# The down projection of a decoder layer: ten sums of weight blocks move from GpSimd to VectorE, and the product of gate and up is made in row halves

## What is computed

```python
h = h + (jax.nn.silu(hn @ W['w_gate'][i]) * (hn @ W['w_up'][i])) @ W['w_down'][i]
gate = jax.nn.sigmoid(rmsnorm(h, W['g_ple'][i]) @ W['w_ple_gate'][i])
h = h + gate * (p[i] @ W['w_ple_proj'][i])
```

## Time and profile before

| | |
|---|---|
| median of 3 runs | 2861.48 us (2856.12 to 2864.07) |
| profiled execution | 2864.79 us, span 2863.0 us |
| busy shares of the span | TensorE 88%, VectorE 48%, ScalarE 25%, GpSimd 21% |
| mean granted TensorE clock | 0.939 of full speed |
| gate and up | about 1808 to 2379 us |
| down | about 2389 to 2698 us |
| embedding stage | about 2698 to 2863 us |

### The profile page before, as it was taken

The page is one execution under the profiler, slowest core; times in us unless marked ns, Lnnn a source line. Parts: engine busy times, 40 slices in busy tenths (PEclk is TensorE's granted clock), DMA queues, the critical chain, the costliest instruction groups (busy, mean ns, idle before and its releaser), DMA issues. The chain is left out here.

```text
span 2863.0 us, 35015 instructions
## 1 busy us (share of the span) xinstructions
PE 2525.2 (88%) x13920; PEld 1741.5 (61%) x13940; DVE 1374.0 (48%) x2301; ACT 706.9 (25%) x1387; POOL 611.8 (21%) x546
## 2 busy tenths in 40 slices
PE   6999999494789997887768779999999998999998
PEld 4555544152578786455445435688888887787743
DVE  0589999342567764586634113422222225334233
ACT  3222220052344453675423200111111110000011
POOL 2000000102544431400056502222122211202000
PEclk9999999695799999898889879999999999999999
DMA  7111101702245443514889843011101104110211
GB/s 267 49 43 45 44 35 40 212 17 75 91 132 170 140 146 116 177 36 148 316 305 344 346 170 103 26 45 45 45 30 45 44 30 143 41 43 1 85 37 36
DMA packets 148459, 305.15 MB, mean 107 GB/s; under 512 B 49784, under 2 KB 99128, under 8 KB 146010
## 3 DMA queue, kind: packets, MB, share of 16 engines
q1 hardware_dynamic: 115986, 169.65, 18.5%
q0 software_dynamic: 25904, 98.19, 9.2%
q10 hardware_dynamic: 6408, 35.08, 3.7%
HBM read 262.23 MB, written 67.77 MB: 115 GB/s over the span
## 5 line engine op out<-in xcount | busy, mean ns | idle before, releaser
L482 PE MATMUL i_psM<-i_w,i_xnT 128*128 128x462 f32 (+2 forms) x1152 | 420.0, 523 | 2.3 <-ACT i_xnT L312 2.3
L482 PEld LDWEIGHTS i_psM<-i_w,i_xnT 128*128 128x128 f32 x1152 | 216.9, 191 | 193.5 <-issue 175.2
L1255 PE MATMUL m_B<-m_big,m_arena 128*128 128x272 f32 x1408 | 328.5, 394 | 4.0 <-DVE m_actT L1019 3.2
L1255 PEld LDWEIGHTS m_B<-m_big,m_arena 128*128 128x128 f32 x1408 | 268.5, 191 | 59.9 <-DVE m_actT L1019 3.4
L1255 PE MATMUL m_B<-m_arena 128*128 128x272 f32 x1056 | 245.9, 393 | 1.8 <-DVE m_arena L1058 1.8
L1255 PEld LDWEIGHTS m_B<-m_arena 128*128 128x128 f32 x1056 | 200.6, 190 | 43.5 <-DVE m_arena L1058 2.2
L889 POOL TENSOR_TENSOR m_arena<-m_arena 128x512 f32<-128x512 f32 x110 | 141.9, 1324 | 386.4 <-DMA m_arena<-w_up 195.9
L1289 PE MATMUL m_B<-m_arena 128*128 128x256 f32 x880 | 200.1, 390 | 23.5 <-DVE m_arena L1119 23.5
L1289 PEld LDWEIGHTS m_B<-m_arena 128*128 128x128 f32 x880 | 172.2, 196 | 50.9 <-issue 26.2
L1085 DVE TENSOR_TENSOR m_actT<-m_actT,m_B 128x544 f32<-128x544 f32 x88 | 60.5, 718 | 215.2 <-PE m_B L1255 215.2
L445 DVE MAX8 l_top<-l_work 128x8 f32<-128x384 f32 (+5 forms) x173 | 150.4, 869 | 5.8
(11 more groups left out here) (427 smaller groups left out, 3939.4 us busy)
## 6 DMA issues: line engine op xcount, KB each, us to landing
b_Kp<-b_k SPq DMA_DIRECT2D x32, 512.0 KB, 11.8
b_Vp<-b_v SPq DMA_DIRECT2D x32, 512.0 KB, 14.6
o_bk<-b_k ACTq DMA_DIRECT2D x8, 2040.0 KB
o_bv<-b_v ACTq DMA_DIRECT2D x8, 2040.0 KB
m_arena<-w_gate SPq DMA_DIRECT2D x11, 1024.0 KB, 5.3
m_arena<-w_up SPq DMA_DIRECT2D x11, 1024.0 KB, 5.4
m_arena<-w_down SPq DMA_DIRECT2D x8, 1408.0 KB, 6.4
i_w<-w_in POOLq DMA_DIRECT2D x5, 1848.0 KB, 35.5
```

The source lines that it names most:

```text
L482: mm = nc.tensor.matmul(psM[:, q % 2, 0:cols.stop - cols.start], xnT[:, t % RING, k, :], w[:, k, cols], start=(k == 0), stop=(k == KO - 1))
L1255: mm = nc.tensor.matmul(B[:, 2 * (q % pairs.SLOTS) + b, 0:QUARTER], stationary(s, m)[:, k, :], moving[m][:, k, b * QUARTER:(b + 1) * QUARTER],
```

## The change

- The ten sums of `w_down` blocks are written into VectorE's stream (`sum_wd_of`). Each stands behind `add(n)` and the activation sum of the first unit (r = 0) of the product group one or more before its use: the sum for product 1 behind the first unit of product 2, for 6 behind 5, for 3 behind 6, for 7 behind 3, for 4 behind 7. GpSimd has none left.
- `moved[6]` is made by VectorE, behind `moved[7]`; GpSimd's weight sums of the second step follow without it.
- In every odd step the product of gate and up is made in two instructions of 128x2x544: row half "2" behind the eviction of product 3, half "1" behind that of product 4. `act_at` counts to 22 instead of 11.
- In the last step nine of the eleven column tiles of the first activation sum are made before row half "2" is multiplied; the remaining two follow the last half.
- The arena is laid out anew: `sil` first, then the sums, then `raw` in two pieces; the two buffers of `sum_act` change places. SP loads block "21" right behind `h1`, and "12", which now lies over `sil`, only once the whole product is made.

```diff
-        raw = arena[:, 6528:10624].rearrange("p (u k f) -> p u k f", u=2, k=KO)
-        summed_w = arena[:, 10624:10624 + pairs.SUMS * KH * P].rearrange("p (u k f) -> p u k f", u=pairs.SUMS, k=KH)
-        sil = arena[:, 14720:14720 + 2 * LIVE].rearrange("p (f r) -> p f r", f=2)
+        sil = arena[:, 6528:6528 + 2 * LIVE].rearrange("p (f r) -> p f r", f=2)
+        summed_w = arena[:, 8704:8704 + pairs.SUMS * KH * P].rearrange("p (u k f) -> p u k f", u=pairs.SUMS, k=KH)
+        raw = [arena[:, o:o + KO * 2 * P].rearrange("p (k f) -> p k f", k=KO) for o in (14848, 12800)]
...
+                load_down(0, "21")
+                sp.wait_ge(act_at, FF_TILES)
                 load_down(0, "12")
-                load_down(0, "21")
...
-                pool.wait_ge(hnT_at, 2 * TILES)
-                nc.gpsimd.tensor_tensor(moved[6], hn["11"], hn["12"], ALU.add).then_inc(moved6_at, 1)
                 for n in range(8, len(pairs.sums)):
                     sum_weights(n)
-                for c in range(2):
-                    for m in WD_SUMS:
...
-                        nc.gpsimd.tensor_tensor(wd[WD_OF[m]], wd[a], wd[b], ALU.add if sign == PLUS else ALU.subtract)\
-                            .then_inc(wd_summed, 1)
...
-                dve.wait_ge(moved6_at, 1)
+                nc.vector.tensor_tensor(moved[6], hn["11"], hn["12"], ALU.add).then_inc(moved_at, 1)
+                dve.wait_ge(moved_at, 3)
                 nc.vector.tensor_tensor(hn["12"], hn["12"], hn["22"], ALU.subtract).then_inc(moved_at, 1)
-                dve.wait_ge(moved_at, 2)
                 nc.vector.tensor_tensor(hn["21"], hn["21"], hn["11"], ALU.subtract).then_inc(moved_at, 1)
...
-                    if s % 2:
-                        dve.wait_ge(silu_at, s // 2 + 1)
-                        dve.wait_ge(accumulated, pairs.dve_after[pairs.step_end(s) - 1])
-                        pair = actT[:, s - 1:s + 1, :]
-                        nc.vector.tensor_tensor(pair, sil[:, :, :], pair, ALU.mult).then_inc(act_at, 1)
+                        if s % 2 and m in (3, 4):
+                            if s == pairs.STEPS - 1 and m == 3:
+                                dve.wait_ge(product_done, pairs.step_end(s - 1))
+                                sum_act_of(0, 0, FH - 2)
+                            dve.wait_ge(silu_at, s // 2 + 1)
+                            dve.wait_ge(accumulated, n)
+                            rows = rows_in["2" if m == 3 else "1"]
+                            pair = actT[:, s - 1:s + 1, rows]
+                            nc.vector.tensor_tensor(pair, sil[:, :, rows], pair, ALU.mult).then_inc(act_at, 1)
...
+                def sum_wd_of(n):
+                    c, m, r = units[n]
+                    if r or m in ("rest", 4):
+                        return
+                    m = {2: 1, 5: 6, 6: 3, 3: 7, 7: 4}.get(m)
+                    if m is None:
+                        return
+                    a, sign, b = WD_SUM_OF[m]
+                    for block in (a, b):
+                        dve.wait_ge(wd_in[block], 16 * (c + 1))
+                    if m in (3, 4):
+                        dve.wait_ge(wd_summed, wd_sum_no(c, m))
+                    nc.vector.tensor_tensor(wd[WD_OF[m]], wd[a], wd[b], ALU.add if sign == PLUS else ALU.subtract)\
+                        .then_inc(wd_summed, 1)
...
-                dve.wait_ge(act_at, FF_TILES // 2)
-                sum_act_of(0)
+                dve.wait_ge(act_at, FF_TILES)
+                sum_act_of(0, FH - 2, FH)
                 sum_act_of(1)
                 dve.wait_ge(h_in, 32)
                 for n in range(NU):
                     add(n)
                     if n + 2 < NU:
                         sum_act_of(n + 2)
+                    sum_wd_of(n)
```

More of the change, by code:

```diff
@@ L699, in weights @@
             i, j = block
-            return raw[:, s % 2, halves[j], P * (int(i) - 1):P * int(i)]
+            return raw[s % 2][:, halves[j], P * (int(i) - 1):P * int(i)]
         def stationary(s, m):
@@ L727, in phase_mlp @@
         product_done, begun_at, accumulated = sem("product_done"), sem("begun"), sem("accumulated")
-        w_summed, moved_at, moved6_at = sem("w_summed"), sem("moved"), sem("moved6")
+        w_summed, moved_at = sem("w_summed"), sem("moved")
         silu_at, act_at = sem("silu"), sem("act")
@@ L896, in _ @@
                             sum_weights(n)
-                pool.wait_ge(hnT_at, 2 * TILES)
-                nc.gpsimd.tensor_tensor(moved[6], hn["11"], hn["12"], ALU.add).then_inc(moved6_at, 1)
                 for n in range(8, len(pairs.sums)):
                     sum_weights(n)
-                for c in range(2):
-                    for m in WD_SUMS:
[L903 to L914, removed]
-                            pool.wait_ge(down_done, end_of(c, "rest"))
-                            pool.wait_ge(wd_summed, wd_sum_no(c, m))
-                        nc.gpsimd.tensor_tensor(wd[WD_OF[m]], wd[a], wd[b], ALU.add if sign == PLUS else ALU.subtract)\
-                            .then_inc(wd_summed, 1)
                 first(N1)
@@ L1058, in _, with sum_act_of @@
                 nc.vector.tensor_tensor(moved[7], hn["21"], hn["22"], ALU.add).then_inc(moved_at, 1)
-                dve.wait_ge(moved6_at, 1)
+                nc.vector.tensor_tensor(moved[6], hn["11"], hn["12"], ALU.add).then_inc(moved_at, 1)
+                dve.wait_ge(moved_at, 3)
                 nc.vector.tensor_tensor(hn["12"], hn["12"], hn["22"], ALU.subtract).then_inc(moved_at, 1)
-                dve.wait_ge(moved_at, 2)
                 nc.vector.tensor_tensor(hn["21"], hn["21"], hn["11"], ALU.subtract).then_inc(moved_at, 1)
+                def sum_act_of(n, f0=0, f1=FH):
+                    if n in act_sum_no:
+                        _, m, r = units[n]
+                        a, sign, b = SUM_OF[m]
+                        nc.vector.tensor_tensor(act_sum(n)[:, f0:f1, :], act_block(a, r)[:, f0:f1, :],
+                                                act_block(b, r)[:, f0:f1, :],
+                                                ALU.add if sign == PLUS else ALU.subtract).then_inc(act_summed, 1)
                 written = {}
@@ L1113, in add @@
                     ins.then_inc(added, 1)
-                def sum_act_of(n):
-                    if n in act_sum_no:
-                        _, m, r = units[n]
-                        a, sign, b = SUM_OF[m]
-                        nc.vector.tensor_tensor(sum_act[:, act_sum_no[n] % 2, :, :], act_block(a, r), act_block(b, r),
-                                                ALU.add if sign == PLUS else ALU.subtract).then_inc(act_summed, 1)
+                def sum_wd_of(n):
[12 more added lines that the diff above has]
+                        .then_inc(wd_summed, 1)
                 def turned_out(t):
@@ L1283, in down @@
                         if m in SUM_OF:
-                            pe.wait_ge(act_summed, act_sum_no[n] + 1)
-                            left = sum_act[:, act_sum_no[n] % 2, :, :]
+                            pe.wait_ge(act_summed, act_sum_no[n] + 2)
+                            left = act_sum(n)
                         else:
@@ L1345, in ple_last @@
                                 mm.then_inc(pp_done, 1)
-                pe.wait_ge(act_at, FF_TILES // 2)
+                pe.wait_ge(act_at, FF_TILES)
                 for n in range(NU):
```

8 lines of the change are left out of this document (5 added, 3 removed).

## The result

| | before | changed |
|---|---|---|
| median | 2860.93 us (2856.12 to 2864.07, 4 runs) | 2841.85 us (2839.11 to 2844.74, 4 runs) |
| ratio | | 0.9935, interval 0.9917 to 0.9953 |
| the same two, five more rounds | 2867.28 us (11 runs) | 2841.45 us (6 runs), 0.9911, interval 0.9895 to 0.9928 |
| profiled execution | 2864.79 us | 2844.74 us, span 2843.0 |

The kernel is faster by 0.65 to 0.9%. Predicted were 2835.3 us, or 0.9%, so direction and range hold, the range with only 1.15 us to spare under its upper end of 2843; the size needs a closer look, since the profiled execution gained only 20.05 us where 26.2 had been summed.

What follows compares the result with a forecast made beforehand. GpSimd's `w_down` sums were taken to lock VectorE out and stall TensorE. Gains 20.6 + 0 + 3.8 + 1.8 = 26.2 us took the profiled 2864.79 to 2838.6, the median 2861.48 to 2835.3 us; range 2828.5 to 2843.

Steps and rivals of the forecast that it cites:

- What bounds the kernel: Down and handover: GpSimd's weight sums lock VectorE out of the shared ports; five TensorE waits, 23.5 us together.
- Part 1: Inside down: with the ten sums off GpSimd, four TensorE gaps vanish; gain 20.6 us.
- Part 2: Down: VectorE takes ten sums of 128x2816 at 3.08 us each, hidden by TensorE's units; cost 0.
- The threshold of 4.5 us: Down: longest weight sum VectorE can take behind a unit before TensorE must wait; 3.08 leaves 1.4 us.
- Part 3: Handover from up to down: TensorE's gap 3.8 instead of 10.37 us, then `h1` comes last; gain 3.8 us.
- rival (a): Handover keeps less (clock low after `h1` stall, 2837.0 us) or gives more (`h1` early, 2832.5); chance 0.20.
- the stall for `h1` exceeds 4 us: Handover: one of three signs that would prove the prediction wrong; it had unit 2 start 2.1 us late.
- Part 4: Start of gate: VectorE makes `moved[6]` too, so TensorE's wait for `moved[7]` goes; gain 1.8 us, bounds 0 and 1.8.
- Part 5: Up and down: halved products, SP's new wait and later loads all cost nothing.
- (b): Down: some gaps stay because weight sums wait in VectorE's in-order queue, 10 us, 2845 us; chance 0.08.
- (d): Down: slower than before, VectorE becomes the bound; with sums of 8 us, 2870 us; chance 0.03.
- (c): Down and handover: the 7.08 us came of something other than GpSimd; only the earlier partial sum helps, 2858 us; chance 0.03.

## Why the prediction was right, and where it was not

**What bounds the kernel.** Right. The line's answer with a median of 1.618 and a maximum of 7.079 was the view that led there. The halved sums on GpSimd confirm the cause. By the Trainium skill (SBUF — State Buffer, section "SBUF: two separate sides") the pair is held for a whole instruction and the other engine blocks fully; 3.85, 3.84 and 3.87 us instead of 2.42 and 1.62 beside halves of the sum agree. (The prediction gave that page's rule too narrowly: beside VectorE's instructions with two SBUF operands it names VectorE's two-port modes. No reading here rests on that.)

**Part 1, the gaps inside down, 20.6.** Measured 20.59. Counting from eviction to eviction took in the low clock; the idle time alone (13.1 us) would have given two thirds.

**Part 2, ten sums at 3.08 us for nothing.** Measured 3.08 each, and no gap. The threshold of 4.5 us measured 4.6 from eviction to eviction and 4.8 by the idle time.

**Part 3, the handover, 3.8.** This is the term that was mis-sized: 1.05 measured. The gap came as worked out (3.46 for 3.8), and that `h1` would be last as well. Two steps inside it failed. The landing was taken from the earlier trace rows, 14.1 + 0.4 = 14.5 us, a row of a kernel in which TensorE stands still for 10 of these us and no code load falls into the transfer; measured 16.17, so unit 2 started 18.60 us after the issue instead of 16.96, 1.6 us late. And the clock: I had units 0 and 1 slow (6.53 + 4.74) and unit 2 warm. They were warm (9.73), which bought nothing, as it only lengthened the stall (2.1 + 1.7 + 1.5 = 5.3; measured 5.44), and that stall brought the clock down, so that unit 2 cost 6.73 us; less the 0.7 us stall that I had before unit 3, and which fell away, that is 1.1 us more than predicted (11.48 from the start of unit 2 to the eviction of unit 3, instead of 10.35). 1.64 + 1.13 = 2.77 account for the 2.75 missing. The clock half of this was rival (a), its upper end, with "the stall for `h1` exceeds 4 us" named as what would prove me wrong: it did. The argument that 2.1 us of stall would leave the clock alone was made for a stall of the wrong length.

**Part 4, the start of gate, 1.8.** Right: 2.04 in the stretch, 1.97 when undone alone. GpSimd's weight sum did get in once, ahead of `moved[6]` and not of `moved[7]` (3.49 us for 2.42), where nobody waits.

**Part 5, nothing.** Right: no gap in up or in the second half, and no wait on a load in down but `h1`.

**Rivals.** (b) and (d) did not occur; one more us on each VectorE sum cost nothing. (c) is refuted by the halved sums. The part of the change that I called a gain of the handover, the row halves and the early partial sum, brought nothing in this kernel: with `h1` last they cannot, and the kernel without them is 1.9 us shorter (with `h1` out of the way they are worth 4.4). I had worked out that `h1` would be last and did not ask what the halves then are worth.

**The total.** The stretch gained 23.68 us, 0.83% of 2864.79; the medians say 0.65% and 0.89% in two measurements. The sum was 26.2. What is missing in the profiled execution beyond Part 3 is 3.9 us ahead of the first gate product. I take them for scatter: for the second profile of the changed kernel I had expected a start between 1806 and 1813, and it started at 1816.96, 5 us from the first. That the median came out within the range is partly luck, since this scatter is larger than the 1.15 us that were left.

## What to carry over

When two engines fight over a port, look for the one instruction whose length is far above its line's median, and count what it costs from eviction to eviction, clock included; cutting the long holder in two is the cheap remedy (19.7 of 23.7 us here). When an edit shortens a handover, list all that the next stage's first step waits for: as soon as one of them is a transfer that starts at a fixed event, everything gained ahead of it is given back, until what doesn't need the transfer is put before the wait on it (6.7 us here). A landing time read from a trace holds for what else ran in that trace, loads of program code included.

## What the runs showed of the hardware

- After an instruction that had been held by GpSimd, VectorE went on with its next one while GpSimd's next, which waited for nothing else, was held: L1121 at 1.61 us behind L1109 at 2.95. Where VectorE waited for a semaphore in between (L1096 of 3.85, then L1121 twice in 6.26), GpSimd got in. The engine that is held does not simply alternate with the other. That the wait in between decides it is read from these places and was not tested.
- The same 3.46 us gap at the same place left the granted clock at 1.00 in five profiles (units 0 and 1 in 9.7 us where the rows show them apart) and brought it to 0.50 in two (11.13 and 11.42 us). The gap's length alone doesn't tell.
- The landing of the same 4352 KB took 14.5 to 14.9 us with TensorE starting 5.7 us or more after the issue (six profiles), and 15.2 to 16.2 with TensorE starting 3.4 us after it (seven), a difference of 1.2 us in the mean. By the Trainium skill (SBUF — State Buffer, "SBUF: two separate sides") a compute operation cannot slow a DMA. These runs don't refute the rule: what differs between the groups is another transfer, a 16 KB load of program code that falls into the seven slower ones and takes 1.1 us.
